# Sample attention with all scores of the next unit ahead of the values of this one, and modulation inside the input projections

## What is computed

```python
mod = silu(c) @ w_ada + b_ada                      # 6 x 1024 values for each of 9 conditionings
shift1, scale1, gate1, shift2, scale2, gate2 = split(mod, 6)
h = x * (1 + scale1) + shift1
qa, ka, va, qb, kb, vb = split(h @ w_in)           # 1024 -> 3072, rotary on q and k
oa = dilated_attention(qa, ka, va)                 # 8 heads x 64, keys at distances of three patterns
ob = diff_attention(qb, kb, vb, lam)               # 4 heads, two maps of 64, value of 128
ob = rms_norm(ob) * 0.8
x = layer_norm(alpha * x + gate1 * (concat(oa, ob) @ w_o))
h = x * (1 + scale2) + shift2
x = layer_norm(alpha * x + gate2 * conv_gated_ffn(h))   # uses state_conv
```

## Time and profile before

| | us |
|---|---|
| runs of the kernel (3) | 1226.54, 1229.12, 1235.38 |
| median | 1229.12 |
| the profiled execution | 1233.46 |
| its span, first to last instruction | 1231.5 |
| PE busy in the span | 1052.7 (85%) |
| DVE, POOL, ACT busy | 839.2, 357.9, 269.5 |
| mean granted TensorE clock | 0.923 of full |

### The profile page before, as it was taken

How to read it: one execution, slowest core, us unless ns; L and a number is a source line. 1 busy time by engine, 2 the same in 40 slices (tenths; PEclk the granted TensorE clock), 3 DMA queues, 4 the chain that set the end, 5 groups by cost and what they waited for, 6 DMA issues and landing times.

```text
span 1231.5 us, 23995 instructions
## 1 busy us (share of the span) xinstructions
PE 1052.7 (85%) x9389; PEld 854.0 (69%) x9389; DVE 839.2 (68%) x1513; ACT 269.5 (22%) x580; POOL 357.9 (29%) x379
## 2 busy tenths in 40 slices
PE   5599999999578677677776996999999999999994
PEld 3377777666455555455555775999999999677772
DVE  1657457167676767667659467567676687998958
ACT  0310010132132223322242104332233222100002
POOL 2333233100000000000016005456565665433323
PEclk9699999999888889778786997999999999999997
DMA  8959895596899999999990215475567731413102
GB/s 303 399 171 327 300 353 174 187 331 220 279 351 344 316 367 322 360 313 343 333 322 1 64 53 195 143 265 207 205 244 274 264 105 69 149 58 106 70 17 77
DMA packets 112549, 276.54 MB, mean 225 GB/s; under 512 B 9608, under 2 KB 33174, under 8 KB 108837
## 3 DMA queue, kind: packets, MB, share of 16 engines
q1 hardware_dynamic: 99125, 250.82, 58.6%
q10 hardware_dynamic: 13312, 24.19, 5.5%
HBM read 264.60 MB, written 76.69 MB: 277 GB/s over the span
## 4 chain that ended last, share of the span: by engine, by line
PE 60%; DVE 18%; DMA 7%; SPq 7%; issue 4%; POOL 2%; ACT 2%; ACTq 0%; DVEq 0%; POOLq 0%; PEldq 0%
PE wide L1576 16%; PE wide L1578 15%; PE wide L1577 15%; DVE ring L1151 3%; PE wide L1650 2%; DMA ring<-in_cache_k 2%; DMA ring<-in_w_ada 2%; PE wide L1639 2%; PE wide L1701 2%; PE wide L1732 2%; DVE ring_r L1083 2%; SPq L598 2%; SPq L433 1%; PE wide L1525 1%; DMA ring<-in_w_down 1%
## 5 line engine op out<-in xcount | busy, mean ns | idle before, releaser
L747 POOL TENSOR_TENSOR ring_r<-ring,ring_r 128x1024 fp32r<-128x1024 f32 x70 | 184.9, 2650 | 271.4 <-DVE ring_r L1043 204.5
L1576 PE MATMUL wide<-x_sb_r,ring_r 128*128 128x288 f32 x704 | 211.4, 300 | 8.2 <-DVE ht_r L1065 5.1
L1577 PE MATMUL wide<-ht_r,ring_r 128*128 128x288 f32 x704 | 209.3, 297 | 0.0
L1578 PE MATMUL wide<-x_sb_r,ring_r 128*128 128x288 f32 x704 | 208.7, 296 | 0.0
L1578 PE MATMUL wide<-ring_r,ht_r 128*128 128x512 f32 (+1 forms) x400 | 158.2, 395 | 0.0
L1151 DVE STREAM_TRANSPOSE ring<-ring 128x512 f32<-128x512 f32 x208 | 129.2, 673 | 20.8 <-DMA ring<-in_cache_k 19.0
L1576 PEld LDWEIGHTS wide<-x_sb_r,ring_r 128*128 128x128 f32 x704 | 133.3, 189 | 11.7 <-issue 11.2
L1578 PEld LDWEIGHTS wide<-x_sb_r,ring_r 128*128 128x128 f32 x704 | 134.2, 191 | 0.0
L1577 PEld LDWEIGHTS wide<-ht_r,ring_r 128*128 128x128 f32 x704 | 133.8, 190 | 0.0
L1576 PE MATMUL wide<-ring_r,x_sb_r 128*128 128x512 f32 (+1 forms) x240 | 97.0, 404 | 10.5 <-DVE ht_r L1065 8.5
L1701 PE MATMUL wide<-ring,x_sb 128*32 128x128 f32 (+1 forms) x1792 | 69.3, 305 | 40.4 <-DVE ring L1151 40.3
(11 more groups left out here) (226 smaller groups left out, 1900.0 us busy)
## 6 DMA issues: line engine op xcount, KB each, us to landing
ring<-in_cache_k SPq DMA_DIRECT2D x128, 256.0 KB
out_wks<-in_cache_win_k SPq DMA_DIRECT2D x8, 4080.0 KB, 19.0
out_wvs<-in_cache_win_v SPq DMA_DIRECT2D x8, 4080.0 KB, 25.3
ring<-in_w_ada SPq DMA_DIRECT2D x12, 2048.0 KB, 10.0
ring<-in_w_up SPq DMA_DIRECT2D x22, 1024.0 KB, 7.6
ring<-in_cache_win_k SPq DMA_DIRECT2D x16, 1024.0 KB
ring<-in_w_in SPq DMA_DIRECT2D x6, 2048.0 KB, 18.4
room<-in_cache_v ACTq DMA_DIRECT2D x32, 256.0 KB
```

Source lines behind the costliest of these rows:

```text
L747: nc.gpsimd.tensor_tensor(rest, w, high.bitcast(F32), ALU.subtract).then_inc(wl_rest, 1)
L1576: nc.tensor.matmul(out, left[0], right[0], start=first, stop=False)
L1577: nc.tensor.matmul(out, left[0], right[1], start=False, stop=False)
L1578: return nc.tensor.matmul(out, left[1], right[0], start=False, stop=last)
```

## The change

- The eight late modulation chunks leave `CHUNKS` and the prompt stage. Each is loaded to a buffer of its own (`late`, 2 MB in `room`, made free by the smaller query tile) and used in the projections: rows ahead of the unit that `LATE_UNIT` names, sums ahead of the one behind it. SyncE loads the next one once the rows of the one before are done. The window copies are issued one by one, by `COPY_UNIT`.
- `NU` is 16: 16 prompt units in the prompt stage, 48 in the sample loop, three per unit (`PER`), each of PE's `prompt_step(y)` doing the values of y-2, the turning of y-1 and the scores of y.
- The queries lie in `qt` without zeros, and the score matmul takes 64 rows.
- PE's order for sample unit w: a prompt step, the turning of w's probabilities, all score groups of w+1 with a prompt step after the second, `score_new(w + 1)`, all value groups of w with a prompt step after the second, the new rows' values. VectorE's and ScalarE's lists follow.
- SyncE issues the first two key groups once section 4 of the projections is done, the key tail after section 5 and the last late chunk; per unit it interleaves the keys of w with the values of w-1. ScalarE issues the key tails of the later windows, and the third and fourth value group of the pages. New rows have one buffer each in place of two. Turned keys and raw keys change places in `ring`, and some small tiles get memory of their own.

The core of the diff (the rest follows from it: semaphore names, masks by mixer, where tiles lie, GpSimd's zeroing of `qtp` gone and that of `kn`, `ktn`, `small` earlier):

```diff
-CHUNKS = [("ada", i) for i in range(4)] + [("in", i) for i in range(6)] + [("ada", i) for i in range(4, 12)] \
+CHUNKS = [("ada", i) for i in range(4)] + [("in", i) for i in range(6)] \
     + [("o", i) for i in range(2)] + [("up", i) for i in range(11)] + [("down", i) for i in range(6)]
-SLOT_OF = [0, 1, 2, 3] + [0, 1] * 3 + [0, 1, 2, 0, 1, 2, 0, 1] + [i % 2 for i in range(19)]
+SLOT_OF = [0, 1, 2, 3] + [0, 1] * 3 + [i % 2 for i in range(19)]
...
+LATE_UNIT = {4: 3, 5: 6, 6: 10, 7: 13, 8: 16, 9: 20, 10: 23, 11: 26}
+COPY_UNIT = {1: (0, "k"), 4: (0, "v"), 8: (1, "k"), 11: (1, "v"), 14: (2, "k"), 18: (2, "v"), 21: (3, "k"), 24: (3, "v")}
...
+        o_all = sb("o_all", [P, 2 * SLOT // 4])
+        small = sb("small", [P, 256])
...
-        qtp = part(room, 0, 8192).rearrange("p (n t) -> p n t", n=16)
-        kt = part(room, 8192, 4096).rearrange("p (f t) -> p f t", f=8)
-        vp = part(room, 12288, 4096).rearrange("p (m t d) -> p t m d", t=TP, m=2)
+        mod_early = ht[:, :, :].rearrange("p k t -> p (k t)")[:, 6 * NT:6 * NT + 2 * CH].rearrange("p (b n) -> p b n", b=2)
+        mod_late = mix[:, 2048:2048 + 2 * CH].rearrange("p (b n) -> p b n", b=2)
+
+        def mod_s(ch):
+
+            return (mod_early if ch < 4 else mod_late)[:, ch % 2, :]
+
+        late = part(room, 12288, KT_D * CH).rearrange("p (k n) -> p k n", k=KT_D)
+        qt = part(room, 0, 4096).rearrange("p (f t) -> p f t", f=8)
+        kt = part(room, 4096, 4096).rearrange("p (f t) -> p f t", f=8)
+        vp = part(room, 8192, 4096).rearrange("p (m t d) -> p t m d", t=TP, m=2)
...
-        kraw = [part(ring, at, 2048).rearrange("p (t d) -> p t d", t=4) for at in (4 * 2048, 5 * 2048, 3 * 2048)]
-        ktg = part(ring, 0, NK * 2048).rearrange("p (b g n) -> p b g n", b=NK, g=16)
+        kraw = [part(ring, at, 2048).rearrange("p (t d) -> p t d", t=4) for at in (0, 2048, 4096)]
+        ktg = part(ring, 6144, NK * 2048).rearrange("p (b g n) -> p b g n", b=NK, g=16)
...
-        NU = 32
+        NU = 16
         pb = pa[NU:]
+        PER = len(pb) // (2 * DB)
...
+            return sa[w][0] == 1 and g >= 2
+
+        def load_key_tail(eng, w):
+
+            G = NG[w] + 2
+            ks = G % NK
+            if G >= NK:
+                eng.wait_ge(kg_t, G - NK + 1)
+            win_k = flat_k[0][sa[w][1]].rearrange("(g r) h d -> g r (h d)", r=16)
+            for i in range(4):
+                eng.dma_start(kraw[ks][32 * i:32 * i + 32, 0:2, :], win_k[96:128, 8 + i:16:4, :]).then_inc(kg_in[ks], 16)
...
+            def load_late(ch):
+
+                if ch > 4:
+                    sp.wait_ge(ada_mm, ch)
+                src = a["w_ada"][0].rearrange("(k p) n -> p k n", p=P)
+                sp.dma_start(late, src[:, :, CH * ch:CH * ch + CH]).then_inc(late_in, 16)
...
-            sp.wait_ge(ada_ok, 4)
-            move_window(0)
+            load_late(4)
...
-                    load_chunk(6 + s)
-                    if s < 3:
-                        move_window(s + 1)
-            for n in range(12, 18):
-                load_chunk(n)
+                    if s < 4:
+                        load_chunk(6 + s)
+                for ch, at in LATE_UNIT.items():
+                    if at == n and ch < 11:
+                        load_late(ch + 1)
+                if n in COPY_UNIT:
+                    i, which = COPY_UNIT[n]
+                    move_window(i, (("cache_win_k", "wks") if which == "k" else ("cache_win_v", "wvs"),))
...
+            load_keys(0, 0)
+            load_keys(0, 1)
+            sp.wait_ge(w_used, CHUNK_AT[("in", 5)] + 1)
+            sp.wait_ge(ada_mm, 12)
+            load_key_tail(sp, 0)
+            for w in range(1, len(sa) + 1):
+                here = len(groups[sa[w][0]]) if w < len(sa) else 0
+                if here:
+                    load_keys(w, 0)
+                    load_keys(w, 1)
+                load_values(sp, w - 1, 0)
+                if here == 4:
+                    load_keys(w, 2)
+                load_values(sp, w - 1, 1)
+                if here == 4:
+                    load_keys(w, 3)
+                if sa[w - 1][0] == 0:
+                    load_values(sp, w - 1, 2)
+                if here:
+                    sp.wait_ge(kn_t, w)
+                    load_new_keys(sp, w)
                 if w >= 2:
-                    sp.wait_ge(kn_t, w - 1)
                     sp.wait_ge(sa_pv, w - 1)
-                    load_new(sp, w)
-
-            for G in range(len(group_list) - 3, len(group_list)):
-                values_behind(G)
+                    load_new_values(sp, w - 1)
...
+                if w + 1 < len(sa) and sa[w + 1][0] == 0:
+                    load_key_tail(act, w + 1)
+                if w:
+                    probs_b(PER * w - 1)
+                    copy_b(PER * w - 2)
+                    take_out(w - 1)
+                if values_by_act(w, 2):
+                    load_values(act, w, 2)
+                probs_b(PER * w)
+                if w:
+                    copy_b(PER * w - 1)
                 act.wait_ge(sa_t, 2 * w + 2)
                 if w >= 1:
                     act.wait_ge(sa_pv, w)
                 full = P * len(groups[m])
                 nc.scalar.activation(pt_s[:, 1, 0:full], bk(3)[:, 0:full], ACT.Copy).then_inc(sa_ph, 1)
-                if values_by_act(w + 1, 0):
-                    load_values(act, w + 1, 0)
-                probs_b(2 * w)
-                if values_by_act(w + 1, 1):
-                    load_values(act, w + 1, 1)
-                if values_by_act(w + 1, 2):
-                    load_values(act, w + 1, 2)
-                copy_b(2 * w)
-                probs_b(2 * w + 1)
-                act.wait_ge(sa_pv, w + 1)
-                nc.scalar.activation(o_s[:, w, :], bk(4)[:, 0:P], ACT.Copy).then_inc(sa_o, 1)
-                copy_b(2 * w + 1)
+                if values_by_act(w, 3):
+                    load_values(act, w, 3)
+                probs_b(PER * w + 1)
+                copy_b(PER * w)
+            probs_b(len(pb) - 1)
+            copy_b(len(pb) - 2)
+            take_out(len(sa) - 1)
+            copy_b(len(pb) - 1)
...
+            jobs += [(n - 0.5, "late_rows", ch) for ch, n in LATE_UNIT.items()]
+            jobs += [(n + 0.55, "late_sum", ch) for ch, n in LATE_UNIT.items()]
...
                 last_g = len(groups[sa[w + 1][0]]) if w + 1 < len(sa) else 0
                 if last_g:
                     turn_keys(w + 1, 0)
+                if w:
+                    mask_b(PER * w - 1)
+                    out_b(PER * w - 3)
+                if last_g:
+                    turn_keys(w + 1, 1)
+                mask_b(PER * w)
+                if w:
+                    out_b(PER * w - 2)
 
                 full = P * len(groups[m])
                 dve.wait_ge(sa_t, 2 * w + 1)
@@ -1276,19 +1326,18 @@
                 dve.wait_ge(sa_t, 2 * w + 2)
                 nc.vector.tensor_copy(ptn[0:32, :, :], bk(4)[0:32, P:3 * P].rearrange("p (h c) -> p h c", h=2)).then_inc(sa_pt, 1)
                 if last_g:
-                    turn_keys(w + 1, 1)
+                    turn_keys(w + 1, 2)
+                mask_b(PER * w + 1)
                 if w:
-                    out_b(2 * w - 1)
-                mask_b(2 * w)
-                if last_g:
-                    turn_keys(w + 1, 2)
+                    out_b(PER * w - 1)
                 if last_g == 4:
                     turn_keys(w + 1, 3)
-                mask_b(2 * w + 1)
...
+                for c, at in LATE_UNIT.items():
+                    if at == n - 1:
+                        ada_sum(c)
+                    if at == n:
+                        ada_rows(c)
...
-                return nc.tensor.matmul(bank[:, 0:P * (qb + 1)], qtp[:, 8 * m + n, P * qb:P * qb + P],
-                                        kt[:, 4 * m + n // 2, 0:P * (qb + 1)], start=True, stop=True)
+                at = slice(64 * (n % 2), 64 * (n % 2) + 64)
+                return nc.tensor.matmul(bank[:, 0:P * (qb + 1)], qt[at, 4 * m + n // 2, P * qb:P * qb + P],
+                                        kt[at, 4 * m + n // 2, 0:P * (qb + 1)], start=True, stop=True)
...
+            def prompt_step(y):
+
+                if y >= 2:
+                    weigh_b(y - 2)
+                if 1 <= y <= len(pb):
+                    turn_b(y - 1)
+                if y < len(pb):
+                    scores_b(y)
...
                 n = 32 * sum(groups[m])
 
-                if w:
-                    weigh_b(2 * w - 1)
-                scores_b(2 * w)
-
+                prompt_step(PER * w)
                 for h in range(2):
                     pe.wait_ge(sa_exp, 2 * w + h + 1)
                     if w >= 1:
@@ -1752,31 +1813,35 @@
                     for u in range(len(groups[m])):
                         src = p_tail[:, h, :] if groups[m][u] == 2 else p_s[:, h, P * u:P * u + P]
                         nc.tensor.transpose(bk(2 + h)[:, P * u:P * u + P], src, perm[:, :])
```

(39 more changed lines are left out.)

181 lines of the change are left out of this document (76 added, 105 removed).

## The result

The changed kernel is slower: its median is 1247.28 us (1234.87 to 1258.49, 14 runs) against 1228.39 us (1224.79 to 1236.58, 14 runs). The ratio is 1.0107, 95% interval 1.0073 to 1.0142, about 13 us; it leaves out four of the 14 that lie over 1.5% above the kernel's fastest, and the profiled execution (1258.49 us, span 1256.7) is one of these, 11 us above the median, so its length isn't all the kernel's. I predicted 1210 us, 1187 to 1238: wrong in sign and outside the range.

The account below looks back on a forecast made before the run. Matmul engine bounds projections and prompt stage, key and value transfers the sample loop. Stream starting 25 us earlier, 6.2 us more to load, loop work 0: -18.8 from the profiled 1233.5 gives 1214.7, against the median 1210 us, range 1187 to 1238.

Parts of the forecast that it names:

- part 2: Prompt stage: keeping 16 of 32 units takes 26.6 us against 67, so -40.4; half-height scores cost nothing.
- rival B: Sample loop: PE becomes the bound with 38 us of added prompt work, +13 us, 1223; chance 0.17.
- Part 1: Projections: modulation chunks 4 to 11 move in and add PE time on the path, +22.9 us, range +20 to +47.
- rival D: Projections: modulation loads come late, held by window copies, +20 us, 1230, no change; chance 0.08.
- the start of the stream: Sample loop's start: page keys go out some 23 us after the projections, at 284, 25 us earlier than 309.
- Part 3: Loop start: key stream begins 25 us earlier, 2.1 MB more left to load costs 6.2 us; together -18.8.
- Part 4: Sample loop: 16 more prompt units, 38 us of PE work, are covered by the new order's saved waits: 0.
- The sign that I named: Sample loop: a right forecast would show 315 to 320 us from the page keys, DMA at 0.97 and over.
- A: Sample loop: the key and value stream runs denser, -20 us more, 1190; chance 0.22.
- C: Sample loop: value buffers given back late block SyncE's queue and starve DMA; 1258 at 3 us per unit; chance 0.10.

Follow-up runs that it names:

- the padded tile: Changed kernel with a zero-padded query tile, filled by GpSimd, so the short prompt stage's 16 score matmuls read 128 rows: ratio 1.0015 to the kernel before.
- the run of the kernel before: Kernel before the change with only its prompt score matmuls cut to the 64 rows of one head: ratio 1.0114 to the kernel before.
- the moved values: Changed kernel, queries padded, first sample unit's three value groups issued behind the key tail, last unit's four by SyncE ahead of w_o: 1218.96 us, ratio 0.9912.
- the old order: Changed kernel with only PE's order put back, scoring a group of the next unit and weighing one of this in turn: ratio 1.0922.

## Why the prediction was wrong, step by step

- **The failing step** is in part 2: "The half-height score matmul (64 rows of the shared query tile in place of 128 with zeros) takes the same columns: I cost it at nothing, between 0 and -1 us." It cost some 11 to 13 us. It costs twice: 0.26 us a unit even at full clock, and the clock, which falls behind the first scores and, once the modulation chunks no longer stand between the prompt units, stays down for nearly the whole stage. Same columns is not same time; and I bounded it only on the side of a gain, where none of the rows that I had read showed a 64-row score matmul at all. The fall of the clock is the larger part: of the 17.6 us that the padded tile brings the page keys forward, 16 units by 0.26 are 4.2, and the other 13.4 go with the clock; the split is an estimate from the run of the kernel before. I had used the granted clock only in rival B, for the loop. This term explains the sign and not the whole miss: the forecast was a ratio of 0.984, and of the 32 us between it and 1.0107 the next steps make the rest.
- **Part 1** (+22.9, range +20 to +47): 31.0, counted from the first projection matmul. TensorE's busy time grew by 25.9 us, 3.0 more than priced (the granted clock of the stage is 0.97 where it was 0.99), and its idle time by 5.1, of which 4.7 are one wait for `w_ada`, rival D at a quarter of its price. Within the range, but 8 us over the value.
- **Part 2 without the half height**, and the start of the stream: I had 23 us from the end of the projections to the page keys. With the clock at 1.00 it is 27.2 (267.49 to 294.66 with all 128 rows, the same when padded), since the first key group is turned half in step 14, as I wrote, and half in step 15 (done at 292.8). With part 1's 8 us, less 2 for a projection stage that began earlier in that execution, the start is at 294 where I wrote 284: mis-sized terms, 10 us. The step of the gain itself is right: at full clock the page keys go out 15 us earlier than before, not 25.
- **Part 3** (+6.2 for the values not loaded yet): right in kind. Issued into the idle stretch, together with the last unit's, they give 10.5 us back, more than I had priced. Alone, without the pad, neither was clear of noise (1.0059 and 1.0125 against 1.0107), so how much is whose stays open.
- **Part 4** (0): holds. With the 16 units more, the padded tile and the moved values, the loop takes the 328.2 us that it took before, for the same bytes (109.1 MB less 2.6 of keys and 2.6 of values issued ahead is 103.9, where 104.3 were left before), and TensorE's 34.6 us of waits for the exponential are 3.9. Without the moved values the loop was 336.3 to 338.9 us in three profiles where part 3 allowed 334.2 (328.0 and 6.2), 2 to 5 us more. The sign that I named, 315 to 320 us from the page keys, doesn't follow from my own sum, which gives these 334.
- **The sum once more**, with the half height repaired: 1212.7 us were predicted for the span; the padded kernel has 1230.7. The 18.0 missing are 10.2 (page keys at 294.24, not 284), 4.7 (loop 338.9, not 334.2) and 3.0 (597.5 behind the loop where before had 594.5; what makes these I didn't find).
- **The rivals.** A did not come: the DMA share fell. (Its ground was read a little high: behind the slow slices has 299 to 393 GB/s and not over 340 throughout.) B's condition (over 280 us busy) was met by none but the old order. C's sign came (36.8 us of stops) without its price: with 30.5 us of them the padded kernel is as fast as before. A reader who stopped at the sign would have named the wrong cause; whether the stops cost the 2 to 5 us of the loop is open. D came small. The cause of the loss was none of my rivals.

The clock stayed at 1.00 as long as this stage's scores ran in all seven profiles that have 128-row scores in it, and fell behind the first scores in all six with 64 rows. That the height lowers it here is shown. Open is why: the pauses don't do it (it fell without the one at the copy and held through a microsecond of standing), the busy column is full only with 64, and half height doesn't rule out the full clock, since the kernel before keeps 1.00 with it once the first chunk has run. What in the chunk's matmuls brings the clock back wasn't tried.

## What to carry to other kernels

A matmul that reads half the rows isn't free of charge: measure it at its place, and if a tile of zeros has to make it full height, that tile may be worth its memory. When a stage is shortened by moving dense matmul work out of it, ask what the clock and the transfers do in what is left: here one fell to half and the others stood idle, and the height restored, with loads issued into that stretch and the last unit's ahead of the weights, turned a loss of 1% into a gain of 1% (medians of 1217 to 1222 us). And a wait that grew after a change is a cause only once a run has taken it away.

## What I had not expected of the hardware

- In 32-bit floats a record of a 64-row matmul with 512 columns took 646 ns and that of a 128-row one 594, both at the full granted clock, and four prompt units took 1.03 us longer with the 64-row ones.
- TensorE was busy 25.00 of 25.00 us at a granted clock of 0.50, and 22.87 of 27.00 at 1.00 with full-height scores in the same work. The Trainium skill (TensorE: Matmul & The Clock Gate, "What's actually happening") says that the clock follows how busy the engine has been; the busy column of the profile is not that measure, by these two rows.
- The spread of times is wider with the low clock: the changed kernel's 14 runs cover 1235 to 1258 us, the 12 with all 128 rows 1223 to 1233 and the padded one's 12 1226 to 1238. Why isn't shown.
